# Two transformer blocks on one core: the weight halves of three boundary chunks made one 128-token block sooner

## The reference, cut to what matters

```python
h = h + rmsnorm(mix, norm_mix_post)                    # mix = mixer @ w_out
z = rmsnorm(h, norm_mlp_pre) @ w_up                    # boundary 0
h = h + rmsnorm(jnp.square(jax.nn.relu(z)) @ w_down, norm_mlp_post)
proj = rms_norm(h, pre_norm_2[0]) @ a_w_in_2           # boundary 1: attention and pooling mixer
h = h + rms_norm(y @ ab_w_out_2, post_norm_2[0])
proj = rms_norm(h, pre_norm_2[1]) @ c_w_in_2           # boundary 2: convolution mixer
```

## Time and profile before

| | us |
|---|---|
| median of three runs (1124.2 to 1126.49) | 1126.48 |
| the profiled execution's own time | 1125.93 |
| its span, first to last instruction | 1124.1 |
| TensorE busy | 1033.6 (92%) |
| VectorE busy | 584.4 (52%) |
| ScalarE busy | 468.5 (42%) |
| mean granted TensorE clock | 0.96 of full |

### The profile page before, as it was taken

The page is one execution under the profiler, slowest core; times in us unless marked ns, Lnnn a source line. Parts: engine busy times, 40 slices in busy tenths (PEclk is TensorE's granted clock), DMA queues, the critical chain, the costliest instruction groups (busy, mean ns, idle before and its releaser), DMA issues.

```text
span 1124.1 us, 12285 instructions
## 1 busy us (share of the span) xinstructions
PE 1033.6 (92%) x4847; PEld 824.7 (73%) x4847; DVE 584.4 (52%) x768; ACT 468.5 (42%) x765; POOL 170.0 (15%) x131
## 2 busy tenths in 40 slices
PE   3899999997999999999999979989898899979897
PEld 2677677886788888888888868767677667657676
DVE  5436665235744234333344463366556397777853
ACT  3325562135533334134123354234355557556541
POOL 2200101000000000000000000022000189886300
PEclk8999999998999999999999999989999799999989
DMA  6532102034221252233224214302033222210301
GB/s 213 73 122 76 38 1 76 1 113 150 76 76 75 75 187 75 75 109 116 76 75 149 76 38 132 141 1 75 2 136 120 68 76 76 75 54 27 145 1 75
DMA packets 55823, 93.91 MB, mean 84 GB/s; under 512 B 2581, under 2 KB 23958, under 8 KB 55638
## 3 DMA queue, kind: packets, MB, share of 16 engines
q1 hardware_dynamic: 53648, 90.61, 23.3%
q10 hardware_dynamic: 2118, 2.52, 1.6%
HBM read 90.76 MB, written 2.36 MB: 83 GB/s over the span
## 4 chain that ended last, share of the span: by engine, by line
PE 55%; DVE 8%; ACT 4%; issue 3%; POOL 1%; DMA 1%; SPq 0%; DVEq 0%; POOLq 0%; ACTq 0%
PE acc L702 17%; PE acc L703 17%; PE acc L704 16%; DVE wlr L1768 2%; ACT wh L1362 2%; DVE psT L2113 1%; POOL pacc L1295 1%; PE psT L861 1%; DMA wl<-in_c_w_in_dram 1%; PE ps L861 1%; PE ps L993 1%; DVE rt L1795 1%; DVE act_lo L1812 1%; ACT junk L1391 1%; PE psT L978 1%
## 5 line engine op out<-in xcount | busy, mean ns | idle before, releaser
L1768 DVE TENSOR_TENSOR wlr<-wl,wh 128x2048 fp32r<-128x2048 f32 (+1 forms) x66 | 149.9, 2276 | 96.4 <-ACT wh L1362 96.4
L702 PE MATMUL acc<-act_hi,wh 128*128 128x512 f32 x464 | 187.9, 405 | 1.7 <-DVE act_lo L1812 1.4
L704 PE MATMUL acc<-act_hi,wlr 128*128 128x512 f32 x464 | 182.3, 393 | 0.0
L703 PE MATMUL acc<-act_lo,wh 128*128 128x512 f32 x464 | 182.1, 392 | 0.0
L1362 ACT ACTIVATE wh<-wl 128x2048 fp32r<-128x2048 f32 (+1 forms) x66 | 123.7, 1880 | 61.2 <-DMA wl<-in_w_up_dram 35.1
L702 PE MATMUL acc<-wh,act_hi 128*128 128x512 f32 x320 | 131.3, 410 | 19.0 <-DVE act_lo L1738 7.6
L703 PE MATMUL acc<-wlr,act_hi 128*128 128x512 f32 x320 | 127.6, 399 | 0.0
L704 PE MATMUL acc<-wh,act_lo 128*128 128x512 f32 x320 | 127.6, 399 | 0.0
L1295 POOL TENSOR_TENSOR pacc<-pacc,prod 128x512 f32<-128x512 f32 x80 | 117.5, 1469 | 28.6 <-ACT prod L1644 16.1
L702 PEld LDWEIGHTS acc<-act_hi,wh 128*128 128x128 f32 x464 | 88.4, 191 | 21.7 <-DVE act_lo L1812 1.8
L703 PEld LDWEIGHTS acc<-act_lo,wh 128*128 128x128 f32 x464 | 88.3, 190 | 19.1 <-issue 1.7
(11 more groups left out here) (221 smaller groups left out, 1536.8 us busy)
## 6 DMA issues: line engine op xcount, KB each, us to landing
wl<-in_w_up_dram SPq DMA_DIRECT2D x16, 1024.0 KB, 6.3
wl<-in_w_down_dram SPq DMA_DIRECT2D x16, 1024.0 KB, 6.3
raw<-in_w_in_dram SPq DMA_DIRECT2D x18, 512.0 KB, 4.8
wl<-in_a_w_in_dram SPq DMA_DIRECT2D x8, 1024.0 KB, 6.2
wl<-in_c_w_in_dram SPq DMA_DIRECT2D x16, 512.0 KB, 6.2
wl<-in_w_out_dram SPq DMA_DIRECT2D x4, 1024.0 KB, 6.2
wl<-in_ab_w_out_dram SPq DMA_DIRECT2D x4, 1024.0 KB, 7.4
wl<-in_c_w_in_dram SPq DMA_DIRECT2D x4, 1024.0 KB, 6.4
```

The lines of the kernel that those rows point to most:

```text
L702: pe.matmul(dst, hi, x_hi, start=first, stop=False)
L703: pe.matmul(dst, hi, x_lo, start=False, stop=False)
L704: return pe.matmul(dst, lo, x_hi, start=False, stop=last)
L1768: dve.tensor_tensor(wlr[slot][:, kk, cols], wl[slot][:, kk, cols], wh[slot][:, kk, cols].bitcast(F32), ALU.subtract).then_inc(wlo_done, 1)
```

## The change

In `boundary_blocks` the two pieces of the following chunk move one block towards the front on both engines. ScalarE makes piece 0 in block 0 and piece 1 in block 1. In boundaries 0 and 1 the `hi` of block 0 stands between `post_scale` and `pre_scale`; in boundary 2 it stands behind `pre_scale`. The `hi` of block 1 stands between the two, as before. VectorE makes piece 0 in block 1 and piece 1 in block 2, at the same place within the block as before. No instruction is added or dropped, and loads and TensorE's order stay.

```diff
@@ ScalarE: boundary_blocks(s, following) @@
                     post_scale(s, b)
-                    if b in (1, 2):
-                        hi(following, b - 1)
+                    if b == 1 or (b == 0 and s < 2):
+                        hi(following, b)
                     pre_scale(s, b)
+                    if b == 0 and s == 2:
+                        hi(following, 0)
@@ VectorE: boundary_blocks(s, following) @@
                     new_resid(s, b)
-                    if b >= 2:
-                        lo(following, b - 2)
+                    if b in (1, 2):
+                        lo(following, b - 1)
                     if b >= 1:
                         lo_turned(s, b - 1)
```

## The result

| | before | after |
|---|---|---|
| median, us | 1125.34 (4 runs, 1124.13 to 1126.49) | 1116.53 (4 runs, 1114.89 to 1120.17) |
| ratio after to before | | 0.9926, 95% interval 0.9897 to 0.9956 |
| profiled execution, its own time / span | 1125.93 / 1124.1 | 1120.17 / 1118.4 |

The change takes 8.3 us by the ratio (5.0 to 11.6 by its interval). The forecast was 7.9. The median of 1116.53 lies under the forecast's own range (1117.5 to 1119.5) and inside the range for 8 in 10 (1115.8 to 1121.0). The profiled execution after is the slowest of its four, so the two spans differ by 5.7 only. To read the parts free of this, I measure each boundary inside one trace, from the turn of block 0 to the turn of block 3 (L840).

The account below looks back on a forecast made before the run. TensorE was taken to bound the kernel, with time won only where it waits, for weights in boundaries 0 and 1. Terms -4.1 - 4.7 + 0.1 + 0.8 = -7.9 us gave a median of 1118.5, range 1117.5 to 1119.5 (8 in 10: 1115.8 to 1121.0).

Parts of the forecast that it names:

- Boundary 0: Turn of block 3 at 306.05 instead of 310.19: 4.1 us less, 2.6 of waiting and 1.5 of slow clock.
- Boundary 1: Turn of block 3 at 670.0 instead of 674.70: 4.7 us less; waits of about 1.7 and 1.9 us stay.
- Boundary 2: Piece 0 in block 0 delays block 1's square; nothing won, 0.8 us lost, between 0 and 1.9.
- The sum: All boundaries: -4.1 - 4.7 + 0.1 + 0.8 = -7.9 us, profiled execution 1118.0, median 1118.5.
- The gain isn't given back behind the boundaries: Behind each boundary: TensorE or a chain from its tiles sets the pace and releases the loads, so the gain stays.
- Rival 1: Boundary 1: clock falls after the second remaining wait, costing 1.6 us; time 1120.1; chance 0.13.
- the forecast of a full clock: Boundary 1: the clock stays full behind the two remaining waits of 1.7 and 1.9 us.
- Rival 2: Blocks' chain slips in boundaries 0 and 1 by the added lo or hi: +1.7 us, time 1120.2; chance 0.09.
- Rival 3: Boundary 2 costs nothing, as its chain finds slack; time 1117.7; chance 0.10.
- Rival 4: Piece 0 lands too late for its earlier hi; zero gain at 11 us landing, 1129.2 at 12; chance 0.03.
- The formula's gains: For landing time L of piece 0: 12.0 - L in boundary 0, 12.2 - L in boundary 1.
- Rival 5: Boundaries 0 and 1: TensorE waits for block 3's activations to the old time; no change, 1126.5; chance 0.03.

Follow-up runs that it names:

- act_only: The changed kernel with VectorE's order as before (pieces in blocks 2 and 3), ScalarE's as changed; one run, 1124.11 us.
- b2_hi_ahead: The changed kernel, but in boundary 2 ScalarE's piece of block 0 stands ahead of pre_scale; one run, 1120.18 us, boundary 2 at 18.65 us.
- b2_as_before: The changed kernel with boundary 2 put back as it was on both engines; 1115.83 us, ratio to before 0.9921.
- dve_only: The changed kernel with ScalarE's order as before (pieces in blocks 1 and 2), VectorE's as changed; 1118.11 us, ratio to before 0.9933.

## Why the prediction was right, step by step

- *Boundary 0, 4.1 us.* 23.16 - 19.03 = 4.13. The stride behind the removed wait is 6.34 as worked out. Normed block 3 came in time, but with 0.11 us in hand where I gave 0.45: in block 3 of the kernel after VectorE's residual waited 0.44 us, for what the trace doesn't name. Not seen by the prediction: 1.5 of the 4.1 hang on a fall of the clock that the same wait doesn't bring every time (act_only). That the trace I started from had that fall is luck for the size of the sum.
- *Boundary 1, 4.7 us, with two waits for normed blocks in its place.* 28.20 - 23.50 = 4.70. The waits are 1.63 and 1.64 us by the brackets, or 1.9 and 1.9 by what the strides of 8.23 and 8.21 have over 6.34; I gave 1.7 and 1.9. Here too a part is clock, 1.7 us by the working at act_only, so that without the fall the gain would be 3.0 (an estimate: 4.70 - 1.7).
- *Boundary 2, 0.8 us lost.* 19.45 - 18.66 = 0.79, with the square of block 1 held up by the piece in block 0. It belongs to that piece's place (b2_hi_ahead), not to moving it. The last of the four transfers took 7.3 us and not 6.9, which is the median of the two in rows 9; issued at 843.9 it landed at 851.2, still 1.0 us ahead of the piece.
- *The sum.* By lengths 4.13 + 4.70 - 0.79 = 8.0 us, forecast 7.9, measured 8.3 by the ratio (5.0 to 11.6). The median 1116.53 lies 2.0 under my 1118.5. Of that, 1.1 is the kernel before itself: its median was 1126.48 when I added up and is 1125.34 beside the kernel after. The other 0.9 is inside the scatter of the runs after (1114.89 to 1120.17).
- *The gain isn't given back behind the boundaries.* Between boundaries 0 and 1 the length is the same, 336.31 and 336.28. The mixer up to boundary 2 takes 181.05 before and 182.25 after, and the end takes 249.69 and 250.27 (from the last turn). These 1.8 us, with the 0.6 by which the first turn came later, are why the profiled spans differ by 5.7 and not 8.0. For the mixer the granted clock goes with it: mean 0.95 in the window above, 0.97 in b2_as_before, which took 179.66 with the same instructions; TensorE's busy time differs by just as much (171.41 and 168.79). Over all nine traces this stretch takes 179.66 to 182.41 us, and 181.05 and 181.08 in the two with the old order on both engines. That this is scatter and not the change is argued from those traces; why the clock falls now in one place and now in another wasn't tried.

```profile
666.36:846.02 179.66, 168.79 (x821) 134.69 (x822) 88.80 (x154) 72.70 (x142) 12.49 (x18) 0.97 0.26 88
```

That line is b2_as_before: length, then busy time and count of TensorE, its weight loads, VectorE, ScalarE and GpSimd, then clock, DMA share and GB/s.

- *Rival 1 (the clock falls behind the waits left in boundary 1).* It didn't: the clock is 1.00 from 640 to 674 us in all six traces in which VectorE's pieces were moved. But my ground against it doesn't hold. I wrote that each wait is shorter than any that a fall followed. In the trace of the kernel before, TensorE waits 1.93 us up to 198.19 and the clock is 0.57 from 200 to 204, and it waits 1.80 and 0.92 us up to 792.29 and 794.92, with 0.57 from 794 to 798. In the trace after, the same wait of 1.93 us left the clock full:

```profile
198.19 1.13 PE L1059 MATMUL acc<-qdec_f,kint_f 64*128 64x128 f32 x8 [1.93 <-DVE S L1949]
...
200.00:204.00 4.00, 4.00 (x12) 0.57 0.00 0
```
```profile
198.57 1.13 PE L1059 MATMUL acc<-qdec_f,kint_f 64*128 64x128 f32 x8 [1.93 <-DVE S L1951]
...
200.00:204.00 4.00, 4.00 (x22) 1.00 0.00 0
```

The first pair is before, the second after, and all instructions up to there are the same. The wait stands in all nine traces; the clock falls within 4 us behind it in six and stays full in three (after, b2_hi_ahead, dve_only). So the forecast of a full clock came true for a reason that I had not found. By the rule cited from the Trainium skill, page "TensorE: Matmul & The Clock Gate", section "What's actually happening", the point of the change shifts from run to run; the page says it of the clock's rise at the start of work. For the fall the traces here show the same: this one wait of 1.93 us has a fall behind it in some executions and none in others.
- *Rival 2 (the chain slips in block 1).* In the kernel after 0.19 us of room was left. In dve_only it was used up, at 0.1 us in boundary 0 and 0.3 in boundary 1.
- *Rival 3 (boundary 2 costs nothing).* False.
- *Rival 4 (the landing decides).* The loads landed in time, so it didn't come about, but as a mechanism it is shown. With the landing 5.5 us later, 10.5 to 10.8 us after the old issue, the kernel is just even with before. The formula's gains, 12.0 - L and 12.2 - L, less the 0.8 of boundary 2, whose load wasn't late, still leave 2 us there, and so it gave 1 to 2 us too small a price for the experiment.
- *Rival 5 (TensorE waits for something else at once).* In part true in boundary 1, where 3.8 us of waits for normed blocks are left, and in neither boundary at the old length.

## What to carry to other kernels

When a wait goes, look for the next thing due at the same place and work out when it is ready: that gave both boundaries to 0.1 us. A gain that holds a slow stretch of the clock behind the wait is sure only for the wait itself: here some 3.2 of the 8.0 us were such a stretch (1.5 and 1.7). Put a moved instruction into a wait that its engine has anyway, and compare the two lengths; the same 1.9 us cost nothing in a gap of 1.58 us for a residual with room behind it, and 0.8 in a gap of 0.90 us on the chain. A first use moved towards its load also spends the load's room, which shows only when the load is late.

## What the runs showed of the hardware

- The fall of the granted clock behind a gap of TensorE isn't settled by the length of the gap: a gap of 1.93 us, the same in nine traces, was followed by half clock in six and by full clock in three; one of 2.37 us was followed by 0.58 for 4 us, one of 2.36 us by full clock. Such a fall makes up 1.5 us of a 4.1 us gain. A stretch of 180 us with the same instructions took 179.66 us at a mean clock of 0.97 and 182.25 us at 0.95.
- The first of two loads of 1 MB, issued 0.4 us apart, landed in 5.0 to 5.3 us in the trace before and in 5.3 and 5.7 us in the trace after. The changed kernel asks for it 1.3 us behind the landing in boundary 0; 3.9 us of waiting appeared when the load came 5.5 us later.
